# Diffusion trunk on one core: in the first projections GpSimd computes the rests of the weights from the third piece on, in place of VectorE

## The reference

```python
def split(h):
    p = h @ w_in                                   # h: tokens x 1024, w_in: 1024 x 2560
    a = p[..., :2 * A_WIDTH]                       # value and gate of the convolution, 512 + 512
    q, k, v = ...                                  # 512 columns each
def conv_module(a):
    u = a[..., :A_WIDTH] * jax.nn.sigmoid(a[..., A_WIDTH:])
    u = depthwise_conv(u, conv_w, conv_b)          # 31 taps
    return jax.nn.silu(layer_norm(u, ln_g, ln_b))
ax, qx, kx, vx = split(hx)
qx = rope_2d(qx); kx = rope_2d(kx)
```

## Time and profile before

| what | value |
|---|---|
| median of three runs | 3603.86 us (3601.70 to 3605.09) |
| time of the profiled execution | 3608.03 us |
| its span | 3606.2 us |
| TensorE (PE) matmul busy | 3320.4 us, 92% |
| VectorE (DVE) busy | 1825.4 us, 51% |
| ScalarE (ACT) busy | 1164.5 us, 32% |
| GpSimd (POOL) busy | 295.0 us, 8% |

### The profile page before, as it was taken

The page is one execution under the profiler, slowest core; times in us unless marked ns, Lnnn a source line. Parts: engine busy times, 40 slices in busy tenths (PEclk is TensorE's granted clock), DMA queues, the critical chain, the costliest instruction groups (busy, mean ns, idle before and its releaser), DMA issues. The chain is left out here.

```text
span 3606.2 us, 47637 instructions
## 1 busy us (share of the span) xinstructions
PE 3320.4 (92%) x18952; PEld 2780.3 (77%) x18952; DVE 1825.4 (51%) x2094; ACT 1164.5 (32%) x1906; POOL 295.0 (8%) x527
## 2 busy tenths in 40 slices
PE   3899589788999999999979698999999899999998
PEld 1787477677888888888869577888887788888886
DVE  4599666455344443444453334555554544444446
ACT  2212165456211111111146323555554322121121
POOL 1000000011000000000012111111111200000001
PEclk6999799989999999999989899999999999999999
DMA  5322596242211111111042743322212221111113
GB/s 183 74 87 93 164 284 234 99 138 83 65 47 35 35 35 35 35 41 41 30 136 84 277 157 94 103 50 55 60 41 83 71 64 57 36 47 58 35 47 116
DMA packets 277081, 316.29 MB, mean 88 GB/s; under 512 B 83824, under 2 KB 222672, under 8 KB 275904
## 3 DMA queue, kind: packets, MB, share of 16 engines
q1 hardware_dynamic: 264160, 267.09, 24.9%
q0 software_dynamic: 12768, 47.08, 3.5%
HBM read 243.54 MB, written 70.58 MB: 87 GB/s over the span
## 5 line engine op out<-in xcount | busy, mean ns | idle before, releaser
L1141 DVE TENSOR_TENSOR y_sum<-ffn_down_ps,y_sum 128x512 f32<-128x512 f32 x396 | 271.3, 691 | 239.4 <-PE ffn_down_ps L90 237.4
L88 PE MATMUL ffn_gate_ps<-y_hi,ring_hi 128*128 128x512 f32 (+1 forms) x880 | 326.0, 370 | 6.9 <-DVEq L1091 6.9
L88 PE MATMUL ffn_down_ps<-ring_hi,ffn_act_hi 128*128 128x512 f32 x792 | 314.3, 397 | 16.8 <-DVE y_sum L1141 10.3
L89 PE MATMUL ffn_gate_ps<-y_lo,ring_hi 128*128 128x512 f32 (+1 forms) x880 | 325.7, 370 | 0.0
L90 PE MATMUL ffn_gate_ps<-y_hi,ring_lo 128*128 128x512 f32 (+1 forms) x880 | 325.5, 370 | 0.0
L89 PE MATMUL ffn_val_ps<-y_lo,ring_hi 128*128 128x512 f32 (+1 forms) x880 | 323.9, 368 | 0.0
L88 PE MATMUL ffn_val_ps<-y_hi,ring_hi 128*128 128x512 f32 (+1 forms) x880 | 323.8, 368 | 0.0
L90 PE MATMUL ffn_val_ps<-y_hi,ring_lo 128*128 128x512 f32 (+1 forms) x880 | 323.7, 368 | 0.0
L89 PE MATMUL ffn_down_ps<-ring_lo,ffn_act_hi 128*128 128x512 f32 x792 | 311.0, 393 | 0.0
L90 PE MATMUL ffn_down_ps<-ring_hi,ffn_act_lo 128*128 128x512 f32 x792 | 310.2, 392 | 0.0
L1071 ACT ACTIVATE ffn_act_hi<-ffn_conv 128x1024 fp32r<-128x1024 f32 x66 | 53.4, 840 | 593.3 <-DVE ffn_conv L1121 593.3
(11 more groups left out here) (315 smaller groups left out, 6974.9 us busy)
## 6 DMA issues: line engine op xcount, KB each, us to landing
da_ada_w<-in_ada_w SPq DMA_DIRECT2D x10, 4096.0 KB, 25.0
out_raw<-in_ffn_w_up SPq DMA_DIRECT2D x44, 512.0 KB, 3.8
ffn_raw<-in_ffn_w_up SPq DMA_DIRECT2D x43, 512.0 KB, 3.8
ffn_raw<-in_ffn_w_down SPq DMA_DIRECT2D x22, 512.0 KB, 6.0
out_raw<-in_ffn_w_down SPq DMA_DIRECT2D x22, 512.0 KB, 5.5
ab_raw<-in_ab_w_in SPq DMA_DIRECT2D x20, 512.0 KB, 3.8
mod_ada_w<-in_ada_w SPq DMA_DIRECT2D x4, 2048.0 KB, 11.2
scratch_mla_q_hi<-up_out_hi POOLq DMA_DIRECT2D x12, 512.0 KB, 2.9
```

Source lines behind the costliest of these rows:

```text
L88: pe.matmul(out, a_hi, b_hi, start=first, stop=False)
L89: pe.matmul(out, a_hi, b_lo, start=False, stop=False)
L1141: dve.tensor_tensor(part, down_ps[:, half, :], part, ALU.add).then_inc(s.sum_done, 1)
```

## The change

VectorE keeps the subtractions of pieces 0 and 1. Those of pieces 2 to 19 move to GpSimd. They stand there in the order of its stores: in each round behind `store_qk(i-1, 1)` come the pieces 4i+2, 4i+3 and 4i+4 (in the last round 14, 15, 16, 17, 18), then `store_conv(i-2)`, `store_qk(i, 0)` and the piece 4i+5 (19 in the last round). VectorE's convolution steps between `gated(i)` and `rotated(i, 0)` become 10 and 3 in every round.

```diff
@@ vector @@
-            def lo(piece, hi_part, dst):
+            def weights(piece):
                 dve.wait_ge(s.hi_done.sem, piece + 1)
-                dve.tensor_tensor(dst, raw[:, piece % 2, :, :], hi_part.bitcast(F32), ALU.subtract)\
-                   .then_inc(s.w_ready.sem, 1)
...
+                dve.tensor_tensor(w_lo[:, piece, :, :], raw[:, piece, :, :], w_hi[:, piece, :, :].bitcast(F32),
+                                  ALU.subtract).then_inc(s.w_ready.sem, 1)
...
-                weights(4 * i + 2)
                 if i:
                     at = convolve(at, 7)
                 gated(i)
...
-                weights(4 * i + 3)
-                if last:
-                    at = convolve(at, 2)
-                    v_weights(0)
-                    at = convolve(at, 4)
-                    v_weights(1)
-                    at = convolve(at, 2)
-                    v_weights(2)
-                else:
-                    at = convolve(at, 8)
-                    weights(4 * i + 4)
+                at = convolve(at, 10)
...
                 rest(i, 0)
-                if last:
-                    v_weights(3)
-                else:
-                    weights(4 * i + 5)
@@ gpsimd @@
+            def lo(piece, hi_part, dst):
+                pool.wait_ge(s.hi_done.sem, piece + 1)
+                pool.tensor_tensor(dst, raw[:, piece % 2, :, :], hi_part.bitcast(F32), ALU.subtract)\
+                    .then_inc(s.w_ready.sem, 1)
...
+            pool.wait_ge(s.w_ready.sem, 2)
             for i in range(AT):
+                last = i == AT - 1
                 if i:
                     store_qk(i - 1, 1)
+                weights(4 * i + 2)
+                weights(4 * i + 3)
+                if last:
+                    v_weights(0)
+                    v_weights(1)
+                    v_weights(2)
+                else:
+                    weights(4 * i + 4)
                 if i >= 2:
                     store_conv(i - 2)
                 store_qk(i, 0)
+                if last:
+                    v_weights(3)
+                else:
+                    weights(4 * i + 5)
```

More of the change, by code:

```diff
@@ L760, in store_v, with weights, v_weights @@
                     .then_inc(v_stored[t % 2].sem, 16)
+            def lo(piece, hi_part, dst):
+                pool.wait_ge(s.hi_done.sem, piece + 1)
+                pool.tensor_tensor(dst, raw[:, piece % 2, :, :], hi_part.bitcast(F32), ALU.subtract)\
+                    .then_inc(s.w_ready.sem, 1)
+            def weights(piece):
+                lo(piece, w_hi[:, piece % 2, :, :], w_lo[:, piece % 2, :, :])
+            def v_weights(j):
+                cols = slice(j * P, (j + 1) * P)
+                lo(4 * AT + j, v_hi[:, :, cols], v_lo[:, :, cols])
+            pool.wait_ge(s.w_ready.sem, 2)
             for i in range(AT):
+                last = i == AT - 1
                 if i:
                     store_qk(i - 1, 1)
+                weights(4 * i + 2)
[6 more added lines that the diff above has]
+                    weights(4 * i + 4)
                 if i >= 2:
```

## The result

The changed kernel takes 3623.65 us (median of four runs, 3620.61 to 3629.59), the kernel before 3604.01 us in the same set. The ratio is 1.0057, 95% interval 1.0040 to 1.0075: slower by 14 to 27 us. The profiled execution has a span of 3622.2 us against 3606.2, 16.0 us more.

The account below looks back on a forecast made before the run. TensorE, 92% busy, was taken as the bound, VectorE nearly level; GpSimd's holds would make VectorE the bound. Stage end +18.6 us, said as +19: 3603.9 + 19 = 3623 us, own range 3613 to 3636, 8 in 10 from 3602 to 3637.

Parts of the forecast that it names:

- The mechanism: Stage of rows 1: GpSimd's SBUF reads block VectorE, delaying the last weight piece and so the v product; +18.6 us, chance 0.66.
- the hold: VectorE's two-SBUF-input instructions blocked for each whole GpSimd subtraction: sixteen times 2.37 us, 37.9 us, up to `rest(3, 0)`.
- the piece behind the stores: Piece 19 on GpSimd follows `store_qk(3, 0)`, which waits for VectorE's `rest`; v product starts at 367.7 us, 24.8 later.
- GpSimd's subtraction: One 128x1024 weight subtraction on GpSimd: 2.37 us, from 2.14 ns an element and 0.18 us fixed.
- The proportional end: Upper end for one GpSimd subtraction: four times the whole 729 ns of the 64x256 one, 2.92 us, giving 3632 us.
- The chain: VectorE's work without reason to wait, from the end of `gated(0)` at 132.63 us to `rest(3, 0)`: 193.9 us without holds.
- The tail: Stage's end: last v store issued at 426.6 us, landed 2.3 us later at 428.9; next stage 2.7 us behind.
- The sum: Stage's last landing moves from 410.3 to 428.9 us, +18.6, said as +19 with smaller waits.
- TensorE's other gaps: TensorE waits before later products, apart from the one near 19 us before the v product: 2 to 4 us.
- Not held: Rival: GpSimd runs beside VectorE, which stops at block 3's first step; v product 348.1 us, time 3603 us; chance 0.25.
- the edits costed at nothing: Moved waits, loads and stores, priced at zero; `store_conv(0)` behind three subtractions would delay block 2's first step if VectorE is free.
- Starvation: Rival: GpSimd's reads pass only when VectorE stops; 18 x 3 = 54 us, time 3658 us; chance 0.05.

## Why the prediction was right, step by step

**The mechanism** was right in both parts, the hold and the piece behind the stores. The hold on VectorE, which the earlier trace rows showed only from GpSimd's side, is there from the other side too. It is gone without reads, nearly doubles with two subtractions (the steps' 33.5 us become 64.8), and appears in the kernel before with reads alone. The rule of the Trainium skill ("SBUF — State Buffer", section "Who interferes with whom") is borne out in both directions: 1.57 us became 3.56 beside a reading GpSimd, and stayed 1.57 beside one that only writes, which the same section says too.

**GpSimd's subtraction:** 2.37 us from the slope and fixed part of the earlier trace rows, 2.40 measured. The proportional end, 2.92, was wrong.

**The hold** was mis-sized. I charged the whole 2.37 us; it is 1.97. A held step ends 1.37 us behind GpSimd where it takes 1.57 alone, so 0.2 us of it run beside GpSimd; and a GpSimd subtraction that had to wait ends 2.22 us behind the start of its turn (164.60 to 166.82) where it takes 2.40 alone, so the other 0.2 us pass while it waits. The sixteen up to `rest(3, 0)` cost 31.5 us instead of 37.9. The chain also began 1.4 us earlier, at 131.2 instead of 132.6: TensorE's first product started 0.3 us earlier and TensorE came to the high clock sooner, which is scatter and not the change. `rest(3, 0)` ends at 355.85 us; the prediction said 364.4. The difference of 8.5 us is 6.4 + 1.4 and 0.7 left over: the other instructions took some 1.6 us less than I had priced them, and a wait of 0.93 us I had not counted.

**The piece behind the stores:** 3.3 us from the end of `rest` to TensorE predicted, 3.8 measured, as that subtraction too waited for a convolution step (2.83 us). The v product begins at 359.66 instead of 367.7. This link is shown by the run that moves the piece.

**The tail** was mis-sized the other way, because its path was wrong. I let the stage end 2.3 us behind the last v store and the next begin 2.7 us later. But GpSimd's order has the last convolution block's two stores behind the last v store, whoever is ready first. They are issued at 419.54 and 420.07, and the next stage begins 8.0 us behind the v store's issue, not 5.0. In the kernel before, 406.30 to 413.01 is the same path. I had read the earlier trace rows by engine and not by queue.

**The sum:** 18.6 us predicted for the next stage's start, 14.0 measured (413.01 to 427.05): -8.0 for the v product's start, +0.5 for the way from there to the last v store (59.35 against 58.9 us), +3.0 for the tail. Two errors of opposite sign cancel in part. The median moved by 19.6 us, and its agreement with the forecast's 19 is partly luck. The interval, 14 to 27 us, holds both. The profiled executions differ by 15.9 us (3608.03 and 3623.93), less than 2 us of it outside the stage and within the scatter seen there; the one of the kernel before was 4.0 us above its median, the one of the changed kernel 0.3. Why executions of one kernel differ by that much is open.

**TensorE's other gaps:** I expected 2 to 4 us before later products; there were 1.3 to 1.7. VectorE fell behind more slowly, by the smaller hold.

**The rivals.** "Not held" came near in its number and not in its path. The kernel without reads begins its v product at 346.6 us (348.1 predicted). But the rival let VectorE wait at block 3's first step, for the store behind pieces 17 and 18; there is no wait there (331.10 us). VectorE waits at block 2's first step, 9.36 us, the place named under the edits costed at nothing. Starvation did not occur: GpSimd waited at most for one VectorE instruction (3.65 us at most, of them 2.2 its own). The row that the prediction held against starvation, 3584.68 us, says less than it took from it: the VectorE instruction that follows there, L1141 at 3584.55 us, reads PSUM, and beside such a one GpSimd is not disturbed anyway.

## What to carry to other kernels

Moving an elementwise instruction with SBUF inputs from a full VectorE to an idle GpSimd was no offload here, where nearly all of VectorE's work reads two SBUF tensors. Each move freed 1.14 us of VectorE and held it for 1.97. Price a move by that difference, and look at what VectorE runs beside it: the products with a PSUM input kept their 0.69 us, and the steps kept their 1.57 us beside a GpSimd that only writes. Before moving anything, look for the queue behind which the one awaited result stands; reordering one piece gave back 11.8 of 14.3 us here, and on the kernel before gained 4.0 us in the stage with no new engine, too little to show in the time of the whole kernel.

## What the runs showed of the hardware that was not expected

- A held instruction's end is GpSimd's end plus a constant: 1.36 to 1.38 us for a 128x1295 step (1.57 alone) over all 17 of the changed kernel, 1.36 behind a copy, 0.69 for the block's first step (0.95 alone), 1.08 for VectorE's own subtraction (1.22 alone).
- That first step has a single tensor input, 128x1295 float32 in SBUF, and is held like the others (3.00 us instead of 0.95). The prediction had not counted it among the held ones. In one row it also delays a GpSimd that only writes: in the kernel without reads the write of 1664 elements takes 1.49 us alone, and 1.87 us at 131.69, where the first step runs until 132.13 us.
- Between VectorE instructions 0.03 us apart GpSimd always got in at the first boundary, even when VectorE's next one was ready. Where GpSimd had two subtractions in a row, a VectorE instruction that was being held went between them: the second, issued at 132.85 us in the kernel that subtracts twice, takes 3.66 us and ends 2.25 us behind the held step, which ends at 134.26.
